# Mixing the last 512 tokens beside the expert turns of the first 512, with the weighted sums as 64x64 corner products

## The chip, the cores and the metric

The kernel runs on one core of one Trainium2 chip. The time is the device time of one launch in microseconds (us), the median of three runs; beside it stands one profiled execution, from which every row below comes.

## The reference

One layer of a hybrid encoder block, batch 1, 1024 tokens, width 1024, float32. It has a token mixer and then a mixture of single-neuron experts (PEER):

```python
h = x @ w_in[l] + b_in[l]                      # conv GLU | q, k, v | two branch gates
y_conv = conformer_conv(h_conv, ...)           # GLU -> causal depthwise conv, 31 taps -> LayerNorm -> silu -> matmul
y_sb = stick_breaking_attention(q, k, v) @ sb_w_o[l]      # 8 heads of 64, strictly causal
mix = (g_conv * y_conv + g_sb * y_sb) @ w_out[l] + b_out[l]
x = layer_norm(DEEPNORM_ALPHA * x + mix, ln1_g[l], ln1_b[l])
# peer, per token and head (8 heads):
s1, s2 = the two halves of (x @ w_q) against 128 keys each; top 16 of each; top 16 of the 256 sums
act = gelu(x . expert_u[idx]);  y += softmax(top)[k] * act[k] * expert_v[idx[k]]      # 16 experts per head
x = layer_norm(DEEPNORM_ALPHA * x + y, ln2_g[l], ln2_b[l])
```

Each of the 1024 tokens picks 8 x 16 = 128 experts, and each expert is a row of 2048 floats (u and v side by side, `uv`), 8 KB.

## The kernel before

Tokens lie in reversed order, in 8 blocks of 128 (one token per partition), so block b attends to the keys of blocks b to 7: block 0 (the last tokens) to eight blocks, block 7 to its own alone. The program is written engine by engine, with semaphores by hand. It has these stages, one after the other:

1. Projections (`split_products`, L171 to L173: each product of two floats as three fp32r products of rounded parts), the depthwise convolution on DVE, and the values.
2. Attention: `UNITS` are the pairs of heads times the blocks, 4 x 8 = 32. For each unit and head, PE makes the scores (L531), ACT two sigmoids (L811, L814), DVE a scan (L1048, `tensor_tensor_scan`, over the unit's width of up to 1024) and a product (L1052), PE turns the result block by block (L546) and multiplies it with the values (L560).
3. Mixing: for each of 8 groups m of 128 output columns and each of two halves h of 512 tokens, PE makes two gates by split products and two branches by plain f32 products (L595); ACT and DVE combine them.
4. `w_out` for block 0 (L607), layer norm 1 (`x1_block`, L1112), queries, scores, top 16.
5. The expert turns: 64 turns (8 blocks x 8 heads) of 8 steps g with two experts each. GpSimd gathers an expert's rows for the 128 tokens of the block with an indirect DMA of 1 MB (L454) into one of 8 slots of `ring`. DVE makes the dot product with x1 (L1173, `dots`) and, in the same turn, the top 16 of the next turn; ACT makes gelu, weight and a diagonal matrix `diag` (L910 to L919, `expert_weights`); PE adds diag x v-row to the block's sum `y` (L649, `experts`), after which the slot is free for the next gather. Turns 0 to 6 also hold `w_out` and layer norm 1 of blocks 1 to 7.

An f32 product of 128x512 shows as two records in the trace (two passes), an fp32r one as one. Names like arena_low and arena_high are the two halves of one big buffer in which nearly all tiles lie; what a row is about is seen from its line. The queue of SP issues the other loads in program order, each behind its semaphore wait.

## Time and profile before

| | |
|---|---|
| median of 3 runs | 3465.28 us (3461.51 to 3466.24) |
| the profiled execution's own time | 3461.93 us |
| its span | 3460.1 us |
| PE, DVE, ACT, POOL busy | 85%, 66%, 36%, 39% of the span |
| moved by DMA | 1134.06 MB, 1073.81 MB of it by the gathers |
| first gather issued, last sum done | 798.1 us, 3449.9 us |

The shares are means over stages with different limits; the table by stage and the rows of single waits say more. A busy PE is not a PE at its peak, since the ends of matmuls are modelled.

### The profile page before, as it was taken

The page shows a single profiled execution, that of the slowest core. Times are in us where ns is not written, and L with a number is a line of the kernel's source. Part 1 is how long each engine was busy: PE and PEld are TensorE (multiplying, and loading weights), DVE is VectorE, ACT ScalarE, POOL GpSimd, SP SyncE. Part 2 cuts the span into 40 slices and gives each one's busy share as a digit, 9 for nine tenths or more (in the row PEclk, how much of TensorE's full clock was granted, in tenths as well). Part 3 has the DMA queues.
Part 4 walks back from the last instruction along what each step waited for, and adds up shares of the span by engine and source line. Part 5 has one row for each costly group of instructions (what it writes and reads, how often), then busy time and mean ns, then how long its engine had stood idle before and what let it go on. Part 6 is the DMA issues. An engine that isn't in the chain of part 4 may idle for free. (4 is left out here: it accounts for less than half of the span.)

```text
span 3460.1 us, 37193 instructions
## 1 busy us (share of the span) xinstructions
PE 2948.2 (85%) x8928; PEld 1540.8 (45%) x8928; DVE 2299.5 (66%) x4699; ACT 1239.6 (36%) x3426; POOL 1356.6 (39%) x1191
## 2 busy tenths in 40 slices
PE   8987799987999788888888888888888888888886
PEld 7754466644444334434333443333434433343432
DVE  6976731115777677676777666777776777777675
ACT  3115621103434343333334333333433333333332
POOL 2400000003434454555554455454445545454553
PEclk9998999998999999999999999999999999999999
DMA  3100011127999999999999999999999999999998
GB/s 147 36 0 19 1 37 44 47 97 319 378 384 382 407 422 422 422 418 412 423 421 419 420 414 422 413 422 421 415 420 421 422 417 421 413 421 419 412 422 339
DMA packets 158049, 1134.06 MB, mean 328 GB/s; under 512 B 17553, under 2 KB 17681, under 8 KB 23442
## 3 DMA queue, kind: packets, MB, share of 16 engines
q0 software_dynamic: 147456, 1073.81, 75.2%
q1 hardware_dynamic: 10514, 59.34, 4.5%
q8 instruction: 32, 0.52, 0.1%
q14 instruction: 47, 0.39, 0.0%
HBM read 1128.88 MB, written 4.19 MB: 327 GB/s over the span
## 5 line engine op out<-in xcount | busy, mean ns | idle before, releaser
L649 PE MATMUL ps<-arena_high 128*128 128x512 f32 x4096 | 1916.7, 614 | 402.9 <-ACT arena_high L919 360.8
L454 POOL DMA_INDIRECT arena_high<-uv_dram,idx_now x1024 | 1225.9, 1197 | 1321.3 <-PE ps L649 1130.0
L1173 DVE SCALAR_TENSOR_TENSOR arena_high<-arena_low,arena_high 128x1024 f32<-128x1024 f32 x1024 | 1239.8, 1225 | 574.4 <-DMA arena_high<-uv_dram,idx_now 561.7
L649 PEld LDWEIGHTS ps<-arena_high 128*128 128x128 f32 x4096 | 766.9, 195 | 1426.5 <-issue 858.0
L910 ACT ACTIVATE gcol<-hcol 128x2 f32<-128x2 f32 x512 | 103.7, 203 | 1200.5 <-DVE arena_high L1173 1200.1
L919 ACT ACTIVATE arena_high<-arena_high,wcol 128x128 f32<-128x128 f32 x1024 | 355.2, 394 | 28.4 <-ACT wcol L912 1.2
L449 POOL CAST idx_now<-arena_high 128x8 uint32<-128x8 f32 x128 | 66.0, 516 | 540.6 <-DVE arena_high L1160 540.1
L912 ACT ACTIVATE wcol<-gcol,arena_low 128x1 f32<-128x1 f32 x1024 | 245.7, 286 | 51.9 <-ACT gcol L910 1.5
L625 PE MATMUL ps<-arena_low 128*128 (+1 forms) x1024 | 236.3, 385 | 5.1 <-DMA arena_low<-w_q_dram 2.9
L625 PEld LDWEIGHTS ps<-arena_low 128*128 128x128 f32 x1024 | 197.5, 193 | 61.0 <-issue 35.0
L173 PE MATMUL ps<-x_hi_bytes,w_bytes 128*128 128x512 f32 x512 | 200.7, 392 | 0.0
L1023 DVE SCALAR_TENSOR_TENSOR arena_low<-arena_low,cols 128x1024 f32 x120 | 177.8, 1481 | 17.5 <-DVE arena_low L1019 0.6
L1072 DVE SCALAR_TENSOR_TENSOR arena_low<-ps,cols,arena_low 128x512 f32<-128x512 f32 x16 | 12.0, 751 | 199.1 <-PE ps L595 199.1
L607 PE MATMUL ps<-arena_low 128*128 128x512 f32 x256 | 116.3, 599 | 7.7 <-DMA arena_low<-w_out_dram 7.7
L1048 DVE TENSOR_TENSOR_SCAN arena_low<-arena_low 128x1023 f32<-128x1023 f32 (+7 forms) x64 | 86.5, 1351 | 42.3 <-ACT arena_low L811 42.3
L595 PE MATMUL ps<-arena_low,arena_high 128*128 128x512 f32 x256 | 112.4, 592 | 0.0
L171 PE MATMUL ps<-x_hi_bytes,w_hi_bytes 128*128 128x512 f32 x256 | 100.9, 394 | 12.2 <-DVE x_lo_bytes L1005 9.0
L171 PE MATMUL ps<-x_hi_bytes,w_bytes 128*128 128x512 f32 x256 | 106.5, 416 | 2.9 <-DVE w_bytes L1064 2.9
L173 PEld LDWEIGHTS ps<-x_hi_bytes,w_bytes 128*128 128x128 f32 x512 | 97.1, 190 | 20.3
L910 ACT ACT_TABLE_LOAD x78 | 100.1, 1283 | 6.4 <-DVE arena_high L1173 5.1
L172 PE MATMUL ps<-x_lo_bytes,w_hi_bytes 128*128 128x512 f32 x256 | 100.6, 393 | 0.0
L172 PE MATMUL ps<-x_lo_bytes,w_bytes 128*128 128x512 f32 x256 | 100.4, 392 | 0.0
(132 smaller groups left out, 2269.3 us busy)
## 6 DMA issues: line engine op xcount, KB each, us to landing
arena_high<-uv_dram,idx_now POOLq DMA_INDIRECT x1024
arena_low<-w_q_dram SPq DMA_DIRECT2D x15, 1024.0 KB, 11.1
arena_high<-w_mix_dram SPq DMA_DIRECT2D x8, 1536.0 KB, 6.3
arena_high<-w_proj_dram SPq DMA_DIRECT2D x16, 512.0 KB, 3.3
arena_high<-xT_dram SPq DMA_DIRECT2D x8, 512.0 KB, 7.6
arena_low<-w_out_dram SPq DMA_DIRECT2D x2, 2048.0 KB, 9.6
arena_low<-x_dram SPq DMA_DIRECT2D x8, 512.0 KB
out_dram<-arena_low SPq DMA_DIRECT2D x8, 512.0 KB
```

Of the source, the lines that this page charges most:

```text
L171: nc.tensor.matmul(out, w_hi, x_hi, start=first, stop=False)
L172: nc.tensor.matmul(out, w_hi, x_lo, start=False, stop=False)
L173: return nc.tensor.matmul(out, w_lo, x_hi, start=False, stop=last)
L454: pool.indirect_dma_start(out=ring[:, s % RING, :], out_offset=None, in_=uv_d, in_offset=bass.IndirectOffsetOnAxis(ap=idx_now[:, s:s + 1], ...
L607: last = nc.tensor.matmul(ps[:, 6 + h, :], mix_blk[:, k, :], w_out[:, k, h * HALF:(h + 1) * HALF], start=(k == 0), stop=(k == KD - 1))
L625: last = nc.tensor.matmul(ps[:, 2, 0:2 * P], x1T[:, k, :], w_q[:, place, k, :], start=(k == 0), stop=(k == KD - 1))
L649: last = nc.tensor.matmul(ps[:, y_bank(b) + h, :], diag[:, s % DIAGS, :], ring[:, s % RING, D + h * HALF:D + (h + 1) * HALF], start=False, ...
L910: steps.link(nc.scalar.activation(gcol[:, s0:s0 + 2], hcol[:, s0:s0 + 2], ACT.Gelu))
L912: last = nc.scalar.activation(wcol[:, s:s + 1], gcol[:, s:s + 1], ACT.Copy, scale=gates_flat[:, bass.ds(t * TOPK + s, 1)])
L919: nc.scalar.activation(diag[:, s % DIAGS, :], ident, ACT.Copy, scale=wcol[:, s:s + 1]).then_inc(diag_ready, 1)
L1023: ins = nc.vector.scalar_tensor_tensor(out=conv[:, c, :], in0=conv_in[:, PAD - k:PAD - k + S], scalar=cols[:, bass.ds(c * TAPS + (C_CW + k ...
L1173: last = nc.vector.scalar_tensor_tensor(out=ring[:, s % RING, 0:D], in0=x1[:, b, :], scalar=1.0, in1=ring[:, s % RING, 0:D], op0=ALU.mult, ...
```

## The change

The first 512 tokens (blocks 4 to 7 of the reversed order) go through attention and mixing alone, and their expert turns start then, as turns 0 to 31. `UNITS` keeps only blocks 4 to 7. Attention for blocks 0 to 3 is done inside turns 11 to 21, five steps to a unit of one pair and one block; their gates and branches in the 52 steps after that (the gates now as plain f32 products instead of three split ones), their `w_out` and layer norm 1 in turns 28 to 30, and their expert turns are 32 to 63. `G` is the number of the step, 8 to a turn. ACT computes the sigmoids of that part as tanh.

The weighted sum changes for all 1024 experts: instead of one 128x128 diagonal times 128x512 per half, an expert takes two 64x64 diagonals on 64 partitions. The even expert of a step uses the corners (lo, lo) and (hi, hi) into PSUM banks 0 and 1, the odd one (lo, hi) and (hi, lo) into banks 2 and 3. At the end of a block the odd sum is copied out by ACT (`odd_out`), swapped and added by PE (`merge`), and read by DVE (`y_out`); the banks are no longer double buffered.

Queries and scores are made for several blocks at a time from `slabs` (2048 query weights and 256 keys per partition, 1.18 MB), which are loaded 21 times in all. The weights `w_mix` and `w_out` are loaded twice, once for each half of the tokens. The first half of the early `w_out` is loaded before mixing ends. The loop over turns is written out.

```diff
-UNITS = [(p, b) for p in range(PAIRS) for b in range(NB)]
+UNITS = [(p, b) for p in range(PAIRS) for b in range(BLK, NB)]
 NU = len(UNITS)
 GROUP = 4
+TURNS = NB * PH
+STEPS = TOPK // 2
+ATT0 = 11 * STEPS
+MIX0 = ATT0 + 84
+OUT0 = MIX0 + 52
+UNIT_STEPS = 5
 
...
+SLABS = [(0, h) for h in range(PH)] + [(0, h) for h in range(5)] + [(1, h) for h in range(PH)]
+
+
...
+def slab_in_turn(t):
+
+    if t < 0:
+        return t + 2
+    if t <= 10:
+        return t + 2
+    return t - 30 + PH + 5 if 30 <= t < 30 + PH else None
+
...
+            def load_w_late(m):
+
+                if m >= 2:
+                    sp_eng.wait_ge(branch_late, m - 1)
+                sp_eng.dma_start(w_mix_late[m % 2], w_mix_d[m, :, :]).then_inc(wmix_late_in[m % 2], 16)
...
+            sp_eng.wait_ge(z_late, 2 * last_unit + 2)
+            sp_eng.dma_start(xT_late, xT_d[:, :, 1, :]).then_inc(xT_late_in, 16)
+            sp_eng.wait_ge(att_late_done, 2 * last_unit + 2)
+            sp_eng.wait_ge(turned_late, 4 * last_unit + 2)
+            load_w_late(0)
+            sp_eng.wait_ge(turned_late, 4 * last_unit + 4)
+            load_w_late(1)
+            load_w_late(2)
+            load_w_late(3)
+            sp_eng.wait_ge(idx_ready, START + 3 * PH)
+            sp_eng.dma_start(x_in[1], x_d[row_of(BLK):row_of(BLK) + P, :]).then_inc(x_loaded, 16)
+            sp_eng.dma_start(b_out_bc[1], b_out_d.partition_broadcast(P)).then_inc(rows_late_in, 16)
+            sp_eng.dma_start(ln1_g_bc[1], ln1_g_d.partition_broadcast(P)).then_inc(rows_late_in, 16)
+            sp_eng.dma_start(ln1_b_bc[1], ln1_b_d.partition_broadcast(P)).then_inc(rows_late_in, 16)
+            load_w_late(4)
+            store_out(2)
+            for m in range(5, KD):
+                load_w_late(m)
+            sp_eng.wait_ge(branch_late, KD - 1)
+            sp_eng.dma_start(w_out_late[1], w_out_d[:, CC:KD, :]).then_inc(wout_late_in[1], 16)
+            sp_eng.wait_ge(gate_late_psum, 2 * KD)
+            sp_eng.dma_start(w_out_late[0], w_out_d[:, 0:CC, :]).then_inc(wout_late_in[0], 16)
+            load_x(BLK + 1)
+            load_x(BLK + 2)
...
-            def experts(b, t, g):
-                for s in range(2 * g, 2 * g + 2):
-                    pe.wait_ge(diag_ready, t * TOPK + s + 1)
-                    for h in range(2):
-                        last = nc.tensor.matmul(ps[:, y_bank(b) + h, :], diag[:, s % DIAGS, :],
-                                                ring[:, s % RING, D + h * HALF:D + (h + 1) * HALF],
-                                                start=False, stop=False, skip_group_check=True)
-                    last.then_inc(expert_used[s % RING], 1)
...
+            def experts(t, g):
+                lo, hi = slice(0, DH), slice(DH, P)
+                e, o = 2 * g, 2 * g + 1
+                pe.wait_ge(diag_ready, t * TOPK + o + 1)
+                for h in range(2):
+                    cs = slice(D + h * HALF, D + (h + 1) * HALF)
+                    for s, rows, out_rows, bank in ((e, lo, lo, h), (e, hi, hi, h), (o, lo, hi, 2 + h), (o, hi, lo, 2 + h)):
+                        last = nc.tensor.matmul(ps[out_rows, bank, :], diag[rows, s % DIAGS, :], ring[rows, s % RING, cs],
+                                                start=False, stop=False, skip_group_check=True)
+                        if h == 1 and rows == hi:
+                            last.then_inc(expert_used[s % RING], 1)
...
+            def merge(pb):
+
+                pe.wait_ge(odd_copied, pb + 1)
+                for h in range(2):
+                    last = nc.tensor.matmul(ps[:, h, :], swap, pre2[:, h * HALF:(h + 1) * HALF],
+                                            start=False, stop=False, skip_group_check=True)
+                last.then_inc(merged, 1)
+
...
+            def stick_scores(u, hd):
+
+                p, b = late_unit(u)
+                w = (NB - b) * P
...
+                r = slice(hd * DH, (hd + 1) * DH)
+                for c0 in range(0, w, HALF):
+                    c1 = min(c0 + HALF, w)
+                    last = nc.tensor.matmul(ps[:, 4 + c0 // HALF, 0:c1 - c0], qT[0][r, p, b * P:(b + 1) * P],
+                                            kT[r, p, b * P + c0:b * P + c1], start=True, stop=True, skip_group_check=True)
+                last.then_inc(z_late, 1)
+
...
+            def late_gates(m, g, k0, k1):
+
+                if g == 0 and k0 == 0:
...
+                for k in range(k0, k1):
+                    o = g * D + k * P
+                    last = nc.tensor.matmul(ps[:, 4 + g, :], w_mix_late[m % 2][:, o:o + P], xT_late[:, k, :],
                                             start=(k == 0), stop=(k == KD - 1))
...
+            def beside(t, g):
+
+                G = t * STEPS + g
+                u, o = divmod(G - ATT0, UNIT_STEPS)
+                if 1 <= u <= PAIRS * BLK and o == 0:
+                    stick_turns(u - 1, 1, 1)
+                if 1 <= u <= PAIRS * BLK and o == 1:
+                    stick_values(u - 1, 1)
+                if 0 <= u < PAIRS * BLK:
+                    if o == 0:
+                        stick_scores(u, 0)
+                    if o == 2:
+                        stick_scores(u, 1)
+                        stick_turns(u, 0, 0)
+                    if o == 3:
+                        stick_turns(u, 0, 1)
+                    if o == 4:
+                        stick_turns(u, 1, 0)
+                        stick_values(u, 0)
+                if MIX0 <= G < OUT0:
+                    m, o = late_mix(G - MIX0)
+                    if o < 4:
+                        late_gates(m, o // 2, CC * (o % 2), CC * (o % 2 + 1))
+                    elif o < 6:
+                        late_branch(m, o - 4)
+                j, o = divmod(G - OUT0, 4)
+                if 0 <= j < BLK:
+                    wout_mm(BLK + j, 2 * o, 2 * o + 2)
+                if 1 <= j <= BLK and o == 2:
+                    transposes(BLK + j - 1)
...
+            def stick_tanh(u, hd):
+
+                _, b = late_unit(u)
+                w = (NB - b) * P
+                i = 2 * u + hd
+                act.wait_ge(z_late, i + 1)
+                if u >= 1:
+                    act.wait_ge(turned_late, 2 * i - 2)
+                else:
+                    act.wait_ge(starts_late_step, 1)
+                nc.scalar.activation(tanh_late[hd][:, 0:w], ps_flat[:, 4 * HALF:4 * HALF + w], ACT.Tanh,
+                                     scale=0.5).then_inc(tanh_done, 1)
+                if u >= 1:
+                    act.wait_ge(stick_late_done, i - 1)
+                act.wait_ge(tanh_done, i + 1)
+                nc.scalar.activation(rest_late[:, hd, 0:w], tanh_late[hd][:, 0:w], ACT.Identity,
+                                     bias=half_col[:, :], scale=-0.5).then_inc(rest_late_done, 1)
+
...
+            def late_stick(u, hd):
+
+                _, b = late_unit(u)
+                w = (NB - b) * P
+                i = 2 * u + hd
+                dve.wait_ge(rest_late_done, i + 1)
+                if i >= 1:
+                    dve.wait_ge(att_late_done, i)
+                nc.vector.tensor_tensor_scan(stick_late[:, 1:w], rest_late[:, hd, 0:w - 1], starts_late[:, 0:w - 1], 0.0,
+                                             ALU.mult, ALU.add).then_inc(stick_late_done, 1)
+                dve.wait_ge(stick_late_done, i + 1)
+                nc.vector.scalar_tensor_tensor(out=tanh_late[hd][:, 0:w], in0=tanh_late[hd][:, 0:w], scalar=1.0,
+                                               in1=stick_late[:, 0:w], op0=ALU.add, op1=ALU.mult).then_inc(att_late_done, 1)
...
+            def beside(t, g):
+
+                G = t * STEPS + g
+                if G == ATT0:
+                    late_starts()
+                u, o = divmod(G - ATT0, UNIT_STEPS)
+                if 0 <= u < PAIRS * BLK and o in (1, 3):
+                    late_stick(u, o // 2)
+                if MIX0 <= G < OUT0:
+                    m, o = late_mix(G - MIX0)
+                    if o == 5:
+                        late_mixed(m)
+                j, o = divmod(G - OUT0, 4)
+                if 1 <= j <= BLK and o == 0:
+                    if j == 1:
+                        dve.wait_ge(rows_late_in, 48)
+                    x1_block(BLK + j - 1)
```

PE in a turn of the last block of before, from the loop body: L633 are the transposes of a query, and the two rows of L649 behind them are one step's sums, two halves of each of two experts.

```order
1297 L633 MATMUL ps<-arena_high,arena_low 128x128 x2
1298 L647 REGISTER_ALU
1299 L649 MATMUL ps<-arena_high 128x512 x2
1300 L647 REGISTER_ALU
1301 L649 MATMUL ps<-arena_high 128x512 x2
```

PE in the changed kernel where the late attention starts: L809 is a step of corner products, L841 the late scores, L853 the turning of the weights, L866 the late values.

```order
977 L809 MATMUL ps<-arena_high 64x512 x8
978 L841 MATMUL ps<-arena_low 128x512 x2
979 L853 MATMUL ps<-arena_high,arena_low 128x128 x4
980 L809 MATMUL ps<-arena_high 64x512 x8
981 L853 MATMUL ps<-arena_high,arena_low 128x128 x4
982 L809 MATMUL ps<-arena_high 64x512 x8
983 L853 MATMUL ps<-arena_high,arena_low 128x128 x4
984 L866 MATMUL ps<-arena_low 64x128 x8
985 L809 MATMUL ps<-arena_high 64x512 x8
```

A step had four products of 128x512 and now has eight of 64x64 corners by 512, with the late work between steps.

DVE in a turn of before, from one pair of dot products (L1173) to the next, with the index part of the top 16 between:

```order
569 L1173 SCALAR_TENSOR_TENSOR arena_high,hcol<-arena_low,arena_high 128x1024 x2
570 L1149 TENSOR_SCALAR top_i<-top_i 128x16
571 L1150 TENSOR_SCALAR pos_ab<-pos 128x16
572 L1151 TENSOR_SCALAR pos_ab<-pos 128x16
573 L1153 TENSOR_TENSOR arena_low<-pos_ab,iota 128x512
574 L1156 TENSOR_TENSOR arena_low<-arena_low,top_i 128x512
575 L1160 TENSOR_REDUCE arena_high<-arena_low 128x16
576 L1173 SCALAR_TENSOR_TENSOR arena_high,hcol<-arena_low,arena_high 128x1024 x2
```

DVE in the changed kernel, the same part inside the late attention: L1486 is the dot product, L1522 the late scan (printed under the name of its instruction class) and L1525 the product behind it.

```order
845 L1522 SCALAR_TENSOR_TENSOR arena_low<-arena_low 128x895
846 L1525 SCALAR_TENSOR_TENSOR arena_low<-arena_low 128x896
847 L1486 SCALAR_TENSOR_TENSOR arena_high,hcol<-arena_low,arena_high 128x1024 x2
848 L1461 TENSOR_SCALAR top_i<-top_i 128x16
849 L1462 TENSOR_SCALAR pos_ab<-pos 128x16
850 L1463 TENSOR_SCALAR pos_ab<-pos 128x16
851 L1465 TENSOR_TENSOR arena_high<-pos_ab,iota 128x512
852 L1468 TENSOR_TENSOR arena_high<-arena_high,top_i 128x512
853 L1472 TENSOR_REDUCE arena_high<-arena_high 128x16
854 L1486 SCALAR_TENSOR_TENSOR arena_high,hcol<-arena_low,arena_high 128x1024 x2
855 L1522 SCALAR_TENSOR_TENSOR arena_low<-arena_low 128x895
856 L1525 SCALAR_TENSOR_TENSOR arena_low<-arena_low 128x896
```

The scans and products that stood ahead of all turns now stand between the dot products of turns 11 to 20, two of each to five steps.

## Rows read from the trace of the kernel before

**Rows 1.** The page: span, busy times, and DMA in 40 slices.

```profile
span 3460.1 us, 37193 instructions
PE 2948.2 (85%) x8928; PEld 1540.8 (45%) x8928; DVE 2299.5 (66%) x4699; ACT 1239.6 (36%) x3426; POOL 1356.6 (39%) x1191
...
DMA  3100011127999999999999999999999999999998
GB/s 147 36 0 19 1 37 44 47 97 319 378 384 382 407 422 422 422 418 412 423 421 419 420 414 422 413 422 421 415 420 421 422 417 421 413 421 419 412 422 339
```

**Rows 2.** By stage: stretch and length, busy of each engine, then granted clock, DMA share, GB/s.

```profile
277.60:456.90 179.30, 134.53 (x1056) 83.53 (x1056) 131.99 (x129) 120.98 (x241) 0.50 (x2) 0.90 0.00 1
456.90:744.30 287.40, 286.07 (x1024) 193.85 (x1024) 49.48 (x61) 35.23 (x47) 0.00 (x0) 0.99 0.10 38
744.30:798.10 53.80, 31.13 (x80) 18.18 (x80) 18.45 (x47) 7.24 (x11) 0.23 (x2) 0.78 0.48 187
798.10:1134.00 335.90, 311.25 (x797) 148.04 (x798) 236.98 (x517) 136.12 (x357) 141.90 (x128) 0.98 0.95 383
1218.00:3431.00 2213.00, 1858.58 (x4766) 869.70 (x4764) 1578.25 (x3654) 842.95 (x2608) 1113.71 (x991) 0.98 1.01 419
```

**Rows 3.** Timeline of the last turn: start, length, engine, line, then idle before.

```profile
3431.27 1.22 DVE L1173 SCALAR_TENSOR_TENSOR arena_high<-arena_low,arena_high 128x1024 f32<-128x1024 f32 x1 [1.25 <-DMA arena_high<-uv_dram,idx_now]
3433.74 1.23 DVE L1173 SCALAR_TENSOR_TENSOR arena_high<-arena_low,arena_high 128x1024 f32<-128x1024 f32 x1 [1.24 <-DMA arena_high<-uv_dram,idx_now]
...
3446.21 3.70 PE L649 MATMUL ps<-arena_high 128*128 128x512 f32 x8 [1.23 <-ACT arena_high L919]
```

**Rows 4.** Who waited for whom, 1218 to 3431 us: total, times, longest.

```profile
POOL arena_high L454 <- PE ps L649: 943.6, 507, 5.3
...
DVE arena_high L1173 <- DMA arena_high<-uv_dram,idx_now: 504.5, 522, 2.2
```

**Rows 5.** Timeline of DVE in the attention stage, second pair of heads and the third's start.

```profile
330.14 2.29 DVE L1048 TENSOR_TENSOR_SCAN arena_low<-arena_low 128x1023 f32<-128x1023 f32 x1 [2.65 <-ACT arena_low L811]
332.46 1.23 DVE L1052 TENSOR_TENSOR arena_low<-arena_low 128x1024 f32<-128x1024 f32 x1
...
351.74 1.49 DVE L1048 TENSOR_TENSOR_SCAN arena_low<-arena_low 128x639 f32<-128x639 f32 x1 [1.38 <-ACT arena_low L811]
353.27 0.83 DVE L1052 TENSOR_TENSOR arena_low<-arena_low 128x640 f32<-128x640 f32 x1
...
357.77 1.22 DVE L1048 TENSOR_TENSOR_SCAN arena_low<-arena_low 128x511 f32<-128x511 f32 x1 [1.42 <-ACT arena_low L811]
...
372.51 2.29 DVE L1048 TENSOR_TENSOR_SCAN arena_low<-arena_low 128x1023 f32<-128x1023 f32 x1 [2.65 <-ACT arena_low L811]
```

**Rows 6.** Timeline of PE in the attention stage, and one stretch of expert sums.

```profile
312.59 1.09 PE L560 MATMUL ps<-arena_low,arena_high 128*64 128x128 f32 x16
313.62 1.13 PE L531 MATMUL ps<-arena_low 64*128 64x512 f32 x4
314.68 1.10 PE L546 MATMUL ps<-arena_low 128*128 128x128 f32 x8
...
1232.05 7.03 PE L649 MATMUL ps<-arena_high 128*128 128x512 f32 x16
```

**Rows 7.** Timeline between mixing and the first gather.

```profile
744.26 0.34 SPq L366 DMA_DIRECT2D arena_low<-w_out_dram  x1
...
751.89 15.61 PE L607 MATMUL ps<-arena_low 128*128 128x512 f32 x32 [7.66 <-DMA arena_low<-w_out_dram]
```

**Rows 8.** Timeline of DVE, the softmax that ends turns 1 and 6.

```profile
894.43 0.16 DVE L1165 RECIPROCAL rden<-den 128x1 f32<-128x1 f32 x1 [0.37 <-ACT arena_high L904]
...
1132.93 0.16 DVE L1165 RECIPROCAL rden<-den 128x1 f32<-128x1 f32 x1 [1.03 <-ACT arena_high L904]
```

**Rows 9.** The page, group of the expert sums: busy, mean ns, idle before.

```profile
L649 PE MATMUL ps<-arena_high 128*128 128x512 f32 x4096 | 1916.7, 614 | 402.9 <-ACT arena_high L919 360.8
```

**Rows 10.** One line's instructions: the read of a finished block's sum.

```profile
L1185 DVE SCALAR_TENSOR_TENSOR arena_low<-arena_low,ps x8: 1215/1217/1222, 1217.6 to 3449.9; 128x1024 f32<-128x1024 f32 x8
```

1246 lines of the change are left out of this document (697 added, 549 removed).

## The prediction

> **What bounds the kernel now.** I read the table by stage first. The reader is to see two programs in it: up to 798 us the DMA moves little (0 to 0.48 of its time) while PE or DVE work, and from 1218 us on the DMA share is 1.01 at 419 GB/s, the same in nearly every slice [rows 1, 2]. A gather moves 128 x 8 KB = 1.049 MB, and at 419 GB/s that is 2.50 us. The timeline of the last turn, where DVE has nothing but dot products, shows it: they start 2.47 us apart, each after a wait for its gather [rows 3]. The waits say the same of the middle: DVE waits 504.5 us in 2213 us for gathers, 9.1 us per turn. GpSimd waits 943.6 us for PE, but that is for a free slot of the ring with gathers still queued, so PE does not bound there [rows 4]. PE is 84% busy all the same (1858.6 of 2213 us): there is no room for mixing beside the old expert sums.
>
> The turns take (3449.9 - 1217.6)/55.4 = 40.3 us each [rows 10]. The first seven take (1132.93 - 894.43)/5 = 47.7 us: there PE is busy 311 of 336 us with `w_out` and queries beside the sums, and DMA falls to 383 GB/s [rows 2, 8].
>
> **The head shrinks.** Attention takes 42.4 us per pair of heads (330.14 to 372.51), and the last four blocks of a pair begin 27.6 us into it (357.77) [rows 5]. Only those four stay ahead of the turns, so 4 x 27.6 = 110, with the wider first unit's lead 112 us go. Mixing is PE-bound (286.1 of 287.4 us) over 16 pieces of 17.9 us, and half stay: -143.5 [rows 2]. Its weights' rounding and splitting now serve one piece instead of two, but DVE and ACT were busy 49 and 35 us of 287, so twice their share stays covered. Between mixing and first gather, 53.8 us, PE waited 7.66 us for `w_out` [rows 7]; its first half is now there, and the transposes of the queries with their copy fall away: -7 (0 if the load of the second half is late instead). The first gather goes from 798.1 to about 536: **-262**, bounds -250 and -268.
>
> **More bytes in the turns.** They are not free when the DMA share is 1.01. Added behind the first gather: 20 slabs of 1.18 MB (23.6), eight `w_mix` (12.6), x for the gates (2.1), both halves of `w_out` (4.2), three rows of norms (1.6), less 14 query weights of 1.05 MB (14.7): +29.4 MB, at 419 GB/s **+70 us**. The lower bound is 40 (some load falls where DVE is the slower), the upper 85.
>
> **The first turns stop being PE-bound.** Their bytes alone, 18.4 MB, take 43.8 us against 47.7, so 7 x 3.9 = **-27**, if PE has the room, which hangs on the corners.
>
> **The corners.** This is the cost that no row shows: four 64x64 products at a time. An f32 product of 512 columns is two records of (7.03 - 0.61)/15 = 0.43 us, so 0.86 us; a step takes four, 3.4 us. The nearest rows are the two halves of what is combined now. L531 makes two such products on different 64 rows of the array into different banks: four records in 1.13 us, where one after the other would take 1.7 and the latency. L560 makes eight products of 128 columns on different 64 output columns, in turn, into one and the same bank: 16 records in 1.09 us against 1.7 and more [rows 6, 9]. So row halves overlap and column halves overlap, nearly whole. I take the four corners as 0.86 us plus little, a step as 1.8 us instead of 3.4. The bounds are 0.86 us for four (a product's own time) and 3.44 us (no overlap), 6.9 us a step.
>
> With that, PE per step, which lasts 5.0 us by DMA: in the late mixing (52 steps) four f32 products (3.4) and the corners, 5.2, but 14.7 MB of weights stretch these steps to 5.6 us by DMA; in chunk queries and `w_out` the same for half of the steps; in late attention some 1.5 + 1.8. DMA stays the bound, narrowly in the mixing. In steps with nothing beside, PE would be busy 1.8 of 5 us. Should the clock granted fall from 0.98 to its lower level (it was 0.78 in the stretch with waits before the first gather [rows 2]), the corners take 3.6 us, as much as the sums take now, and the DMA covers that too.
>
> **Late attention on DVE.** A head's scan and product cost 3.52 us at width 1024 and 2.32 at 640 [rows 5], 2.92 on average, and 32 of them 93 us, in ten turns (80 steps). The idle of DVE there is 10 x 9.1 = 91 us. So DVE and DMA tie. Behind a late scan stand the next dot products, behind those the weights, the sums, and the free slot, and the ring of eight absorbs only part of the lag. I take **+20**, between 0 and 60. ACT gets tanh, scaling and copies, some 5 us to a unit of 25 us, with 62% idle (843 of 2213 us busy): 0, covered by that idle; the order of its instructions has no table load at the tanh.
>
> **Small ones.** Seven block ends now pass ACT copy, merge, read and clearing in series before PE goes on, some 5 us that the ring mostly covers; DVE waits for scores of chunks; layer norms of four late blocks in 16 steps; more instructions to load, since the turns are written out. Together **+15** (0 to 40). The end gets copy and merge before the last read: **+3**.
>
> **Sum.** 3460.1 - 262 + 70 - 27 + 20 + 15 + 3 = 3279 us of span. The profiled execution's own time is 1.8 us above its span, and the median 3.4 above that: **3284 us**, 5.2% less. The likeliest case alone reaches from 3235 to 3335.
>
> **Rivals.**
> Pairs of corners exclude each other. In L531 the two row halves wrote to different banks, in L560 the same bank was shared by products that used the same rows. The corners (lo, lo) and (hi, hi) use different rows and one bank, which neither row covers. If they take turns, four corners cost two products, 1.72 us, and a step 3.4 as now. Then PE bounds the late mixing (6.8 us a step instead of 5.6, some +50 over 52 steps), `w_out` (+20), the first turns (+10), the chunk queries and attention (+10 each): 3284 + 100 = 3385. For it: nothing in the trace; against it: the one bank in L560.
> The Trainium skill, TensorEngine Tiling (Array Packing), "Restrictions and Gotchas", states exactly this rule: different row tiles cannot access the same PSUM bank at once. By it the sum would be 3385, by the rows 3284; this trace has no case of it.
>
> The late attention holds the turns. Each head passes PE, ACT twice, DVE twice, PE, ACT, PE in fixed steps, between dot products that tie with the DMA. If lags don't heal, its turns take 45 to 47 us rather than 42: +40 to +50, 3330. For it: the tie of 93 against 91 us; against it: a chain that is spread over five steps of 5 us.
>
> The corners do not overlap at all. Every step then takes 6.9 us on PE, 512 steps 3530, and the end is at 536 + 3530 + 15, some 4080 us, slower by 18%. It decides from here: outside the sums PE has about 590 us of other work behind the first gather (165 late gates and branches, 118 late attention, 96 `w_out`, 168 chunk queries, the rest transposes, scores and merges), so the old end is reached at (2914 - 590)/512 = 4.5 us a step, 2.27 us for four corners, 1.5 of them at a time. L531 and L560 stand against it with nearly two at a time each.
>
> **Chances.** The likeliest case 0.68, exclusive pairs 0.14, held by late attention 0.12, no overlap or something else as large 0.06. Range: 3225 to 3400 holds the first three but for their tails, some 0.85. Faster by over 0.2%, which is about what three runs can tell from no change: 0.93, within 0.2%: 0.01, slower 0.06.
>
> **What the profile of after would show.** First gather near 536 us. DMA share near 1 from then to the end, and some 1163 MB moved. Eight corner products (16 records) in about 1.8 to 2 us; 3.4 us would be the exclusive pairs, 6.9 no overlap. PE's busy share in the last 26 turns about 40%. Turns of 43 to 44 us at the start, 41 to 42 in late attention, some 45 in late mixing, 40.3 in the last 26. In late attention DVE without long waits for gathers. The prediction is wrong if the DMA share falls well below 1 over many turns, or if the steps beside mixing wait for PE.

## The result

| | before | after |
|---|---|---|
| median | 3465.28 us | 3285.16 us (4 runs, 3283.15 to 3287.93) |
| ratio to before | | 0.9482, 95% interval 0.947 to 0.9494 |
| span of the profiled execution | 3460.1 us | 3281.3 us |
| first gather, last sum | 798.1, 3449.9 us | 523.2, 3271.6 us |
| head; expert phase; rest | 798.1; 2651.8; 10.2 us | 523.2; 2748.4; 9.7 us |

The kernel got 5.2% faster. The head lost 274.9 us and the expert phase gained 96.6.

The page of the changed kernel, to be laid beside [rows 1] and [rows 9]:

```profile
span 3281.3 us, 37294 instructions
PE 2446.8 (75%) x12464; PEld 998.8 (30%) x12464; DVE 2297.7 (70%) x4704; ACT 1159.3 (35%) x3326; POOL 1326.3 (40%) x1197
...
PEclk9998997888888898889999999997777777777777
DMA  3101226999999999999999999999999999999997
GB/s 142 39 0 65 77 104 272 396 413 420 421 420 405 410 409 375 409 420 410 397 397 419 394 409 412 421 419 421 409 421 421 420 398 421 421 421 402 421 421 313
DMA packets 162792, 1163.71 MB, mean 355 GB/s; under 512 B 17857, under 2 KB 17985, under 8 KB 26178
...
L809 PE MATMUL ps<-arena_high 64*64 64x512 f32 x8192 | 1275.3, 749 | 724.2 <-ACT arena_high L1163 721.2
```

The gathers start three slices earlier than in [rows 1]. Behind that the reader sees more slices below 421 GB/s: a stretch from the 13th to the 25th, and then one slice in four. The expert sums were 4096 records and 1916.7 us and are 8192 records and 1275.3 us.

The same by stage (stretch and length, busy of PE, PEld, DVE, ACT, POOL, then granted clock, DMA share, GB/s). The first three rows are attention, mixing and what lies between mixing and first gather, as in [rows 2]. The next eight are the blocks of eight turns, cut where the line that reads a finished sum starts, and the last is all of them:

```profile
279.70:331.30 51.60, 38.02 (x296) 23.48 (x296) 41.48 (x66) 38.29 (x102) 0.00 (x0) 0.88 0.02 7
331.30:475.30 144.00, 143.94 (x512) 97.43 (x512) 31.74 (x36) 23.66 (x30) 0.00 (x0) 0.99 0.18 66
475.30:523.20 47.90, 28.61 (x109) 19.66 (x109) 18.13 (x45) 3.86 (x7) 0.19 (x1) 0.79 0.39 148
...
523.20:890.40 367.20, 285.84 (x1496) 109.78 (x1496) 248.89 (x560) 131.79 (x399) 159.41 (x153) 0.87 1.00 411
890.40:1225.90 335.50, 260.04 (x1529) 106.30 (x1529) 273.86 (x573) 155.83 (x437) 162.36 (x143) 0.89 1.00 411
1225.90:1588.30 362.40, 284.17 (x1563) 111.86 (x1563) 279.07 (x577) 158.10 (x435) 163.92 (x146) 0.91 1.00 405
1588.30:1960.00 371.70, 338.78 (x1528) 121.66 (x1528) 267.50 (x588) 141.18 (x404) 156.29 (x145) 0.96 0.99 401
1960.00:2299.00 339.00, 256.47 (x1320) 85.31 (x1320) 230.10 (x536) 121.18 (x388) 151.59 (x144) 0.88 1.01 418
2299.00:2623.30 324.30, 188.71 (x1033) 43.84 (x1032) 230.42 (x536) 108.05 (x356) 162.01 (x144) 0.74 1.01 418
2623.30:2947.50 324.20, 186.68 (x1032) 43.42 (x1032) 230.69 (x536) 108.05 (x356) 157.69 (x144) 0.75 1.01 415
2947.50:3271.60 324.10, 184.25 (x1032) 42.99 (x1032) 219.28 (x498) 105.30 (x348) 147.28 (x134) 0.77 0.97 400
523.20:3271.60 2748.40, 1984.93 (x10532) 665.15 (x10532) 1979.81 (x4402) 1029.49 (x3120) 1260.54 (x1151) 0.85 1.00 410
```

The kernel before, cut the same way (its read of a sum stands 22 us behind a block's end, so the cuts are moved by that), first block, fourth block, and the whole phase:

```profile
798.10:1195.60 397.50, 359.63 (x926) 172.25 (x927) 273.05 (x593) 157.30 (x416) 166.21 (x151) 0.97 0.96 386
...
1839.20:2161.40 322.20, 269.73 (x699) 126.56 (x698) 230.68 (x536) 123.33 (x380) 160.46 (x144) 0.98 1.01 419
...
798.10:3449.90 2651.80, 2249.13 (x5760) 1054.30 (x5760) 1878.16 (x4309) 1014.80 (x3066) 1291.58 (x1151) 0.98 1.00 413
```

Read together: the first block went from 397.5 to 367.2 us. The second to fifth went from 322 each to 335.5, 362.4, 371.7 and 339.0. These are the blocks beside which the late tokens are mixed, scored and loaded. The last three are about 2 us longer than before.

The last steps of the program on PE (start, length, engine, line, idle before it), which answer to [rows 3] and [rows 6]:

```profile
3255.09 1.95 PE L809 MATMUL ps<-arena_high 64*64 64x512 f32 x16 [1.29 <-ACT arena_high L1163]
3260.05 2.58 PE L809 MATMUL ps<-arena_high 64*64 64x512 f32 x16 [3.01 <-ACT arena_high L1163]
3264.98 3.45 PE L809 MATMUL ps<-arena_high 64*64 64x512 f32 x16 [2.35 <-ACT arena_high L1163]
3269.61 1.98 PE L825 MATMUL ps<-arena_high 128*128 128x512 f32 x4 [1.18 <-ACT arena_high L1172]
```

A step of eight corner products (16 records) takes 1.95 us where the granted clock is 1.00 (the level of 2.4 GHz) and 3.45 us where it is 0.55 (nearly all of it at the level of 1.2 GHz). Steps start 4.9 to 5.0 us apart, so PE is idle for 1.5 to 3 us of each.

### The profile page after: what moved, and what is told of

The parts are those of the page before. It is cut to its first block and busy times, and to the rows that moved or that the text cites. A ratio compares the mean times of both kernels' runs of the same rounds, so it can differ in the third digit from the quotient of the medians.

```text
span 3281.3 us, 37294 instructions
## 1 busy us (share of the span) xinstructions
PE 2446.8 (75%) x12464; PEld 998.8 (30%) x12464; DVE 2297.7 (70%) x4704; ACT 1159.3 (35%) x3326; POOL 1326.3 (40%) x1197
## 2 busy tenths in 40 slices
DMA packets 162792, 1163.71 MB, mean 355 GB/s; under 512 B 17857, under 2 KB 17985, under 8 KB 26178
## 5 line engine op out<-in xcount | busy, mean ns | idle before, releaser
L809 PE MATMUL ps<-arena_high 64*64 64x512 f32 x8192 | 1275.3, 749 | 724.2 <-ACT arena_high L1163 721.2
L1486 DVE SCALAR_TENSOR_TENSOR arena_high<-arena_low,arena_high 128x1024 f32<-128x1024 f32 x1024 | 1237.2, 1224 | 631.4 <-DMA arena_high<-uv_dram,idx_now 620.8
L809 PEld LDWEIGHTS ps<-arena_high 64*64 64x64 f32 x8192 | 308.3, 156 | 1567.7 <-ACT arena_high L1163 1101.6
L1163 ACT ACTIVATE arena_high<-arena_high,wcol 128x64 f32<-128x64 f32 x1024 | 300.4, 340 | 16.7
L1156 ACT ACTIVATE wcol<-gcol,arena_high 128x1 f32<-128x1 f32 x1024 | 245.7, 287 | 16.8
L778 PE MATMUL ps<-arena_low 128*128 128x512 f32 (+1 forms) x512 | 223.5, 580 | 0.0
L1331 DVE SCALAR_TENSOR_TENSOR arena_low<-arena_high,cols,arena_low 128x1024 f32<-128x1024 f32 x120 | 183.9, 1533 | 4.3
L211 PE MATMUL ps<-x_hi_bytes,w_bytes 128*128 128x512 f32 x384 | 151.0, 393 | 0.0
L778 PEld LDWEIGHTS ps<-arena_low 128*128 128x128 f32 x512 | 93.9, 194 | 140.9 <-issue 124.3
L1486 DVE DVE_READ_ACCUMULATOR arena_high<-arena_low,arena_high 128x1 f32 x1024 | 83.8, 82 | 0.0
L881 PEld LDWEIGHTS ps<-arena_low 128*128 128x128 f32 x256 | 47.7, 196 | 76.8 <-issue 76.7
L1522 DVE TENSOR_TENSOR_SCAN arena_low<-arena_low 128x1023 f32<-128x1023 f32 (+3 forms) x32 | 60.4, 1887 | 14.3 <-ACT arena_low L1194 13.9
```

Of the source, the lines that this page charges most:

```text
L211: return nc.tensor.matmul(out, w_lo, x_hi, start=False, stop=last)
L778: last = nc.tensor.matmul(ps[:, 4 + half, j0 * P:j1 * P], w[:, k, half * P:(half + 1) * P], x1T[:, j0:j1, k, :], start=(k == 0), stop=(k = ...
L809: last = nc.tensor.matmul(ps[out_rows, bank, :], diag[rows, s % DIAGS, :], ring[rows, s % RING, cs], start=False, stop=False, skip_group_c ...
L881: last = nc.tensor.matmul(ps[:, 4 + g, :], w_mix_late[m % 2][:, o:o + P], xT_late[:, k, :], start=(k == 0), stop=(k == KD - 1))
L1156: last = nc.scalar.activation(wcol[:, s:s + 1], gcol[:, s:s + 1], ACT.Copy, scale=gates[:, t % (BLK * PH), s:s + 1])
L1163: nc.scalar.activation(diag[:, s % DIAGS, :], ident64, ACT.Copy, scale=wcol[:, s:s + 1]).then_inc(diag_ready, 1)
```

## The experiments

Eleven kernels were made from the changed one, and the changed one was run once more in the last group, beside the three that differ from it by a few us. The two kernels of the next section ran once each, the others four or five times. A gain or loss in us is counted from the changed kernel's first median, 3285.16 us, where nothing else is said.

### Two corners at a time, and one

Both products of the odd expert go where those of the even one go:

```
-  ((e, lo, lo, h), (e, hi, hi, h), (o, lo, hi, 2 + h), (o, hi, lo, 2 + h))
+  ((e, lo, lo, h), (e, hi, hi, h), (o, lo, lo, h), (o, hi, hi, h))
```

> The odd expert of a step goes through the same two corners and into the same banks as the even one, so that two corners are in use and not four; the sum is the same. If all four corners of the changed kernel work at once (16 records of a step in 1.95 us at full clock, in its trace), a step's records should now take about twice that, 3.4 to 3.9 us at full clock. Theory A (the gathers set the time from the first gather to the end): TensorE has room for it while a turn of 8 steps is at 40.5 us, and only beside the late attention and mixing, where it is busy most of the time already, does it cost something: 3285 to 3330 us in all. Rival B (TensorE sets the pace wherever other work stands beside the experts): 512 steps by 1.7 us less what idle time it had, 3385 us or more. Rival C (the two corners that share a bank were not at once before either): 3285 us and 1.95 us a step as before.

And all of them through one corner (the high 64 rows of the sums are left out; both experts' slots are freed behind their last product):

```
-  ((e, lo, lo, h), (e, hi, hi, h), (o, lo, hi, 2 + h), (o, hi, lo, 2 + h))
+  ((e, lo, lo, h), (e, lo, lo, h), (o, lo, lo, h), (o, lo, lo, h))
...
+                for s in (e, o):
+                    done[s].then_inc(expert_used[s % RING], 1)
```

> All products of a step go through the one corner of the low rows and low columns; the high 64 rows of the gathered data and of the sums are left out. It is the ruler for the corners: nothing overlaps, so 16 records of a step should take 16 by 0.43 us = 6.9 us at full clock, against the 1.95 us of the changed kernel with four corners. Then TensorE is the bound through all 512 steps: 523 + 512 x (6.9 to 7.5) + 10 = 4070 to 4370 us. If products of 64 rows in the same corner overlap or take less than 0.43 us each, it is nearer 3300 us.

Measured, in one run each: 3494.95 us with two corners, 4827.45 us with one. A step on PE, with two corners (timeline):

```profile
3101.05 3.65 PE L809 MATMUL ps<-arena_high 64*64 64x512 f32 x16 [1.14 <-ACT arena_high L1163]
```

and with one:

```profile
3103.86 7.08 PE L810 MATMUL ps<-arena_high 64*64 64x512 f32 x16
```

The same 16 records take 7.08, 3.65 and 1.95 us with one, two and four corners: 1.94 times and 3.6 times as fast. In the two-corner kernel (lo, lo) and (hi, hi) use different rows of the array and always the same bank. If these two took turns, that kernel would have shown 7 us. So the corners are free of each other, a shared bank included, and the ruler of the second expectation (6.9 us for one corner) holds.

The two-corner kernel also says what the corners are worth to the whole change. Its step of 3.65 us is as long as the old one, whose 8 records took 3.70 us [rows 3], and with late attention and mixing beside the turns it needs 3494.95 us, more than the 3465.28 us before the change. By this run the move without the shorter sums would have gained nothing.

The times were far above theory A's 3285 to 3330 us, and above the 4070 to 4370 us for one corner. By blocks (starts of the read of a finished sum, differences in us; the first counts from the first gather at 523.2 us of the changed kernel):

| block | 1 | 2 | 3 | 4 | 5 | 6 | 7 | 8 |
|---|---|---|---|---|---|---|---|---|
| changed kernel | 367 | 335.5 | 362.4 | 371.7 | 339.0 | 324.3 | 324.2 | 324.1 |
| two corners | 411 | 351.8 | 402.9 | 449.6 | 369.2 | 326.5 | 324.8 | 324.8 |
| one corner | 607 | 555.8 | 586.7 | 656.5 | 548.4 | 445.1 | 446.7 | 446.5 |

With two corners the last three blocks cost nothing, as theory A has it: 3.65 us still fits in a step. The first five cost 44, 16, 41, 78 and 30. Beside the late attention PE is then the bound (stretch, then busy of PE first):

```profile
1015.00:1430.00 415.00, 396.20 (x1865) 157.82 (x1864) 338.44 (x682) 198.71 (x527) 200.42 (x170) 0.99 0.97 382
```

It is busy 396 of 415 us and the gathers fall to 382 GB/s. The changed kernel is busy 285.84 of 367.2 us in its first block and 338.78 of 371.7 in its fourth; 64 steps by 1.7 us more, 109 us, fit in neither, nor in the 75 to 83 us that it idles in the second, third and fifth. In each of the last three it idles 136 us or more. So rival B of this expectation (TensorE sets the pace wherever other work stands beside the experts) is right for five blocks and theory A for three.

### More bytes

Twelve loads of the size of a late slab, which nobody reads, in turns 41 to 52:

```
+            for n in range(12):
+                sp_eng.wait_ge(idx_ready, START + 41 + n)
+                sp_eng.wait_ge(slab_in, 16 * (len(SLABS) + n))
+                sp_eng.dma_start(slab[1], slabs_d[n % PH, :, :]).then_inc(slab_in, 16)
...
```

> Twelve loads of the size of a late feature slab (14.2 MB in all), whose data nobody reads, are added in the turns 41 to 52, after the late mixing is done. Theory A (bytes set the time there): 14.2 MB by 1/419 GB/s, about +34 us, 3319 us. Rival B (the pace of a turn is set by an engine or a gather's own latency, and the DMA engines have slack): under +10 us. Rival D (the loads disturb the gathers by more than their bytes): +45 us or more.

Measured: 3319.20 us (3315.62 to 3321.34), ratio 0.9585 (0.9569 to 0.9601), +34.0 us. The sixth and seventh blocks grew from 324.3 and 324.2 to 345.4 and 338.3 us, the eighth did not (322.9). Bytes cost there what 419 GB/s make of them.

### Fewer weights in the late mixing

```
+                n = 3 * D if m < 2 else P
-                sp_eng.dma_start(w_mix_late[m % 2], w_mix_d[m, :, :])
+                sp_eng.dma_start(w_mix_late[m % 2][:, 0:n], w_mix_d[m, :, 0:n])
```

> Of the late copy of the mixing weights only 128 of 3072 columns are loaded from the third group on (6 loads of about 1.5 MB less; the products read what the buffer held before, so the mixed values of the last 512 tokens are not the reference's). Theory A (bytes set the time of the late mixing, 306 us for 52 steps): 9.1 MB by 1/419 GB/s, about -21 us, 3264 us. Rival B (TensorE or ScalarE set it there): within 5 us of the changed kernel.

Measured: 3284.26 us (3282.54 to 3289.43), ratio 0.9492 (0.9477 to 0.9508): no change. First the stretch of the late mixing in the changed kernel, then in this one:

```profile
1465.00:1780.00 315.00, 289.91 (x1244) 100.57 (x1245) 202.08 (x451) 111.47 (x325) 125.83 (x118) 0.96 1.00 405
```

```profile
1465.00:1780.00 315.00, 291.19 (x1252) 100.86 (x1248) 202.88 (x459) 110.19 (x326) 129.01 (x120) 0.96 0.97 379
```

The rate falls from 405 to 379 GB/s, 8.2 MB in 315 us, and the time stays. The late mixing is not bound by bytes, and theory A fell. (Six loads are cut to 128 of 3072 columns each.)

### Half of the late gates

```
-                for k in range(k0, k1):
+                for k in range(k0, k1, 2):
```

> The late gates are made with half of their products (every second block of 128 features is left out, so the mixed values of the last 512 tokens are not the reference's). Theory A (the late mixing, 306 us for 52 steps, goes at the pace of the bytes): within 5 us of 3285 us. Rival B (TensorE sets the pace there, since it has gates and experts in the same steps): about -30 to -45 us, 3240 to 3255 us.

Measured: 3277.35 us (3271.03 to 3278.65), ratio 0.9455 (0.9441 to 0.947), -8 us. The stretch:

```profile
1465.00:1780.00 315.00, 254.36 (x1167) 82.09 (x1168) 214.06 (x486) 115.43 (x341) 138.87 (x126) 0.93 1.01 421
```

Two groups of instructions say how long the mixing itself took, the late gates and the branches: first and last start in the changed kernel, with durations,

```profile
L881 PE MATMUL ps<-arena_low x256: 592/592/1220, 1468.9 to 1764.7; 128*128 128x512 f32 x128
L895 PE MATMUL ps<-arena_low x128: 592/592/697, 1491.1 to 1775.7; 128*128 128x512 f32 x128
```

and with half of the gates:

```profile
L881 PE MATMUL ps<-arena_low x128: 592/592/1220, 1468.9 to 1748.2; 128*128 128x512 f32 x128
L895 PE MATMUL ps<-arena_low x128: 592/592/697, 1487.7 to 1759.7; 128*128 128x512 f32 x128
```

The mixing took 290.8 us in place of 306.8, and now it goes at 421 GB/s. So neither expectation was met: PE bounds it in the changed kernel, with the DMA 16 us behind, and half of the gates is more than it takes to change the bound.

Only 8.4 of these 16 us are left at the end of the fourth block. Most of the others are lost again in the late `w_out` products that stand right behind the mixing, first in the changed kernel, then in this one:

```profile
L739 PE MATMUL ps<-arena_low x128: 592/592/697, 1778.6 to 1870.3; 128*128 128x512 f32 x128
L739 PE MATMUL ps<-arena_low x128: 592/592/697, 1765.9 to 1861.0; 128*128 128x512 f32 x128
```

From the last branch to the last of these it is 94.6 us in the changed kernel and 101.3 with half of the gates. One reason can be read from the bytes. During its mixing the changed kernel moved 124.17 MB, this one 122.35; the 1.8 MB, 4.3 us at 421 GB/s, are gathers that ran ahead into the ring while PE was the bound, and that this kernel has still to make. The blocks behind the fourth are together 5 us longer in this trace, the slowest of the four executions; why, it doesn't show.

### A short scan in the late attention

```
-  tensor_tensor_scan(stick_late[:, 1:w], rest_late[:, hd, 0:w - 1], starts_late[:, 0:w - 1], ...)
+  tensor_tensor_scan(stick_late[:, 1:64], rest_late[:, hd, 0:63], starts_late[:, 0:63], ...)
```

and the product behind it in the same way.

> The scan and the product behind it of the late attention cover 64 columns in place of up to 511 (the rest of the weights is left out, so the late half is not the reference's). Theory A' (VectorE sets the pace beside the late attention, 5.31 us a step against 5.06 us a step in the undisturbed turns; about 77 steps): -15 to -20 us, 3265 to 3270 us. Rival B' (the gathers and the late scores' own loads set it there): within 4 us of the changed kernel. Rival C' (TensorE, which also makes the late scores, sets it): within 4 us too, and the idle time of VectorE in 1015 to 1430 us is then put down to TensorE.

Measured: 3274.13 us (3266.64 to 3276.28), ratio 0.9454 (0.944 to 0.9469), -11 us. The stretch in the changed kernel and in this one:

```profile
1015.00:1430.00 415.00, 320.55 (x2004) 136.93 (x2000) 370.39 (x731) 215.62 (x568) 211.90 (x178) 0.90 0.99 402
```

```profile
1015.00:1430.00 415.00, 322.27 (x2072) 138.39 (x2070) 306.64 (x751) 219.85 (x582) 204.15 (x185) 0.92 1.01 416
```

Who waited for whom there (total, times, longest), two lines of the changed kernel and the same two of this one:

```profile
ACT gcol L1154 <- DVE arena_high L1486: 168.5, 56, 7.2
DVE arena_high L1486 <- DMA arena_high<-uv_dram,idx_now: 18.2, 18, 2.6
...
ACT gcol L1154 <- DVE arena_high L1486: 162.5, 68, 4.9
DVE arena_high L1486 <- DMA arena_high<-uv_dram,idx_now: 93.1, 93, 2.2
```

DVE was busy 370.4 of 415 us in the changed kernel, and the gathers went at 402 GB/s. With 64 us of scan taken away they go at 416. ACT's wait for the dot products is about the same in both and tells nothing; DVE's own wait for gathers does: 18 us with the full scan, when the data were nearly always there first, and 93 us without it. PE has the same work in both (320.6 and 322.3 us), so rival C' is out. Theory A' holds in kind: what the late attention costs the turns is DVE's time. Its size, 15 to 20 us, is less sure. The late mixing starts at 1449.9 us in place of 1468.9, and the execution in the trace ended 16.5 us before that of the changed kernel; but it is the fastest of the four, and by the medians the gain is 11.

### The clock

```
+                    if t >= 38:
+                        for _ in range(7):
+                            nc.tensor.matmul(ps[:, 7, :], zeros[:, 0:P], zeros[:, :], start=True, stop=True, ...)
```

> From turn 38 on TensorE makes seven products of zeros more in each step (128 x 512, bf16, into a bank that nothing uses then), so that it is not idle long enough for its granted clock to fall to 0.7 to 0.8. Theory A (the fallen clock costs nothing, since the gathers set the pace): the same time within 3 us, with a granted clock near 1.0 in the last third. Rival B (the low clock lengthens the part of a step that is on the path): -5 to -15 us. Rival C (the added products delay the expert products behind them): +5 us or more.

Measured: 3286.58 us (3280.81 to 3288.35), ratio 0.9483 (0.9469 to 0.9498). The last third in the changed kernel and in this one:

```profile
2260.00:3250.00 990.00, 568.14 (x3152) 132.07 (x3144) 698.36 (x1615) 329.18 (x1088) 484.93 (x439) 0.76 1.01 417
```

```profile
2260.00:3250.00 990.00, 718.85 (x4520) 224.00 (x4516) 700.03 (x1622) 328.73 (x1086) 504.64 (x440) 0.98 1.01 417
```

The granted clock goes from 0.76 to 0.98 and neither rate nor time moves. A step's sums at the lower clock are hidden too, and the fallen clock is free.

### What a block's end costs

The last three blocks take 324.2 us, and the sixth and seventh go at 418 and 415 GB/s where single slices reach 421: 2.3 and 4.6 us of each are below full rate. Four kernels looked for them. The first, in its core, has banks of its own for every second block from the sixth on, and the last sum of a block stands behind the first step of the next:

```
+def y_bank(pb):
+    return 4 if pb in (5, 7) else 0
...
+                    if own and t % PH == 0 and g == 1:
+                        merge(t // PH - 1)
```

> From the sixth block of expert turns on, every second block sums into the banks 4 to 7, which the late mixing has left free by then, and the closing of a block (merge, the copy of the odd half, the last sum) stands behind the first step of the next block and not ahead of it. Theory A (a turn is 39.8 us by its bytes, and the closing of a block makes some 4.5 us of every 324 us in which the gathers wait for buffers): -9 to -13 us for the three block ends, 3272 to 3276 us. Rival B (the buffers of the gathers cover the closing, and 40.5 us a turn is the pace of the DMA engines): within 3 us of 3285 us.

Measured: 3288.33 us (3283.31 to 3295.42), ratio 0.9495 (0.9482 to 0.9508). No gain where theory A had 9 to 13 us: what PE's wait for the last sum costs is too little to measure, as rival B had it. The trace of the changed kernel then showed another thing. Here is DVE (third of the busy times) and the rate (last column) 27 us before a block's end at 2947.5 us, and in the 40 us behind it:

```profile
2920.00:2930.00 10.00, 7.38 (x32) 1.60 (x32) 7.08 (x13) 5.47 (x15) 2.66 (x4) 0.50 1.02 423
...
2950.00:2960.00 10.00, 6.78 (x48) 1.61 (x40) 9.55 (x29) 2.54 (x10) 3.26 (x4) 0.83 0.99 388
2960.00:2970.00 10.00, 5.12 (x36) 1.26 (x32) 8.42 (x18) 6.90 (x16) 4.43 (x5) 0.83 0.97 367
2970.00:2980.00 10.00, 3.12 (x24) 0.81 (x18) 9.45 (x16) 3.91 (x12) 3.15 (x4) 0.73 1.01 416
2980.00:2990.00 10.00, 6.49 (x48) 1.82 (x44) 5.30 (x14) 2.54 (x10) 5.82 (x7) 0.84 0.93 354
```

DVE is busy 84 to 96% for 30 us behind the block's end, with the read of the sum, the choice of the next experts and the closing norm, and in three of four slices the gathers fall to 354 to 388 GB/s. The next kernels act on the norm. One leaves most of it out at three block ends:

```
+                w = 16 if 4 <= pb < NB - 1 else D
```

> The norm that closes a block covers 16 of 1024 columns for the fifth to the seventh block (the other columns are stored without it), which takes some 4 us of VectorE out of the fifth step after each of these three block ends. Theory N (a block takes 324.2 us and not 320 because VectorE is 93 to 96% busy in the 40 us behind its end, where the norm stands beside the choice of the next experts, and dots come late, so that the gathers fall from 421 to 350 to 400 GB/s): -6 to -12 us for the three, 3273 to 3279 us. Rival S (the store of the block and its writes cost the DMA engines that time): within 2 us of the unchanged kernel. Rival B (the wait of TensorE for the last sum costs it): within 2 us too.

The other cuts it in four, a piece to each of the steps 4 to 7:

```
-                    if t % PH == 0 and t >= 1 and g == 4:
-                        finish(t // PH - 1)
+                    if t % PH == 0 and t >= 1 and g >= 4:
+                        finish_part(t // PH - 1, g - 4)
```

> The norm that closes a block is cut into four pieces, one in each of the steps 4 to 7 of the turn behind the block's end, where VectorE has only the two dots (about 2.6 of 5.06 us). Theory N: -1 to -2.5 us for each of seven block ends, -5 to -15 us, 3270 to 3280 us. Rival S or B: within 2 us of the unchanged kernel.

The last has both, the cut norm and the own banks, with the sum's read moved to step 4:

```
+                    if t % PH == 0 and t >= 1 and g == (4 if own else 0):
                         y_out(t // PH - 1)
```

> As the kernel with the cut norm, and from the sixth block on each second block has banks of its own, so that the last sum of a block waits until step 4 of the next turn and the norm follows in the steps 5 to 7; nothing of a block's end then stands beside the choice of the next experts. Theory N: 3 to 6 us less than the kernel with the cut norm alone (two to three block ends by 1 to 2 us each), 3265 to 3277 us. Rival B (only TensorE's wait counts): the cut norm alone gives nothing and this one gives 3 us, as own banks alone did in their last block.

And the changed kernel beside them:

> The changed kernel itself once more, as the ruler for the three kernels beside it, which differ from it by a few us only: 3285 us within 3 us.

| | median | runs | ratio to before |
|---|---|---|---|
| changed kernel again | 3288.02 | 3280.61 to 3293.95 | 0.9492 (0.9476 to 0.9509) |
| norm left out at three ends | 3285.26 | 3282.34 to 3288.60 | 0.9486 (0.9473 to 0.9499) |
| norm cut in four | 3277.12 | 3274.88 to 3281.89 | 0.9466 (0.9453 to 0.9479) |
| cut, own banks, later read | 3275.79 | 3272.45 to 3280.19 | 0.9459 (0.9446 to 0.9472) |

Cutting the norm gives 11 us, 0.33%, as expected, against the repeated kernel (8 against the first four runs; its slowest run, 3281.89 us, overlaps the fastest of the repeated kernel). But the kernel without the norm at three ends gives 3, not 6 to 12, which is less than its spread. The stretch behind the fifth block's end has the dip in the repeated kernel,

```profile
2299.00:2349.00 50.00, 26.17 (x159) 6.76 (x161) 39.79 (x95) 17.17 (x52) 20.54 (x20) 0.77 0.96 383
```

and without the norm it has none:

```profile
2299.00:2349.00 50.00, 29.14 (x160) 7.36 (x164) 37.22 (x97) 18.44 (x58) 21.68 (x23) 0.79 1.01 422
```

The block is stored inside this stretch in both (the store is issued at 2326.9 and 2324.7 us), so at this end the store is not the cause (rival S). In the 50 us behind the two other ends the rate is 391 and 412 GB/s without the norm and 375 and 378 with it. Measured against 421 GB/s, the three stretches together lose 15 us with the norm and 5 without. Yet the sixth, seventh and eighth blocks take 326.5, 321.4 and 324.7 us, against 326.8, 325.3 and 323.7 in the repeated one: one end gives 3.9 back and the two others nothing. So a dip of the rate is not yet time of the kernel, and most of the 10 us that the dips lost less are lost elsewhere. Nor do single blocks tell much here: the sixth took 324.3 us in one execution of the changed kernel and 326.8 in the other. The blocks of the kernel with the cut norm say where its gain is. The third takes 359.5 us against 362.8 and the fourth 367.9 against 372.8, where PE or DVE bound anyway; from the fifth on it is 1.7, 2.7, 1.3 and -1.2. So the norm's place costs something, and by this one pair of traces most of it in the loaded blocks. What the ends of the last three cost is not settled. The own banks add 1 us to the cut norm, not the 3 to 6 expected, and that is nothing measurable.

## Why the prediction was right

**The time** came out 1.2 us from the forecast, which is partly luck: the head gave 13 us more than I summed and the expert phase took 16 more.

**The head: -262 forecast, -274.9 measured.** Mixing gave 287.4 - 144.0 = 143.4 us against 143.5, and what lies behind it 53.8 - 47.9 = 5.9 against 7. The wait of 7.66 us for `w_out` [rows 7] is gone:

```profile
477.52 14.00 PE L739 MATMUL ps<-arena_high,arena_low 128*128 128x512 f32 x32 [2.24 <-DVE arena_low L1388]
```

The mis-sized term is the attention, "112 us go". Mixing starts at 331.3 us in place of 456.9, so 125.6 went. A pair of heads takes 11.9 us, from the first scan to the next pair's:

```profile
292.35 1.22 DVE L1356 TENSOR_TENSOR_SCAN arena_high<-arena_high,arena_low 128x511 f32<-128x511 f32 x1 [1.37 <-ACT arena_high L1051]
...
304.24 1.22 DVE L1356 TENSOR_TENSOR_SCAN arena_high<-arena_high,arena_low 128x511 f32<-128x511 f32 x1 [1.37 <-ACT arena_high L1051]
```

I had left it the 14.8 us that the last four blocks took before [rows 5]. In them were waits of DVE for ACT of 1.48, 0.27 and 2.65 us, the last before the next pair's wide start; now they are 0.27 and 1.37. I had carried an interval over with its waits in it.

**Bytes: +70 forecast.** The page has 1163.71 MB, as forecast (1163). In the turns it is 410 x 2748.4 against 413 x 2651.8 us, 31.7 MB more, which at 421 GB/s is +75. The extra loads confirm the price, +34.0 us for 14.2 MB.

**The rest of the expert phase** is time in which the DMA engines ran below full rate. Worked out as length by (1 - rate/421): before 33 us in the first block, 8 in the next six and 10 in the last; after 8.7, 8.0, 13.8, 17.7, 2.4, 2.3, 4.6 and 16.2, together 74 against 51, so +23. With the bytes that is +98, against 96.6 measured. My terms for it were -27, +20, +15 and +3, together +11; the bytes gave 5 more than their +70.

- *The first turns, -27*: 33 - 8.7 = 24 us went. The step holds, and it does hang on the corners: with two of them the block takes 44 us more.
- *Late attention on DVE, +20*: DVE and DMA tie, as I wrote, and the short scan shows it from DVE's side with 11 us. The size holds too: 402 in place of 421 GB/s over the 415 us is 19 us. From the first late score (1015.2 us) to the first late gate (1468.9) it is 84 steps at 43.2 us a turn. That lies between my 41 to 42 and the 45 to 47 us of the rival "the late attention holds the turns", which did not come.
- *The step that failed* is "DMA stays the bound, narrowly in the mixing", with 5.6 us a step. PE was the bound at 5.9 us: six smaller loads changed nothing, fewer products did, and with half of the gates the steps took the 5.6 us (290.8/52) that I had for the bytes. The error is small in time, 0.3 us in 52 steps, 16 us, and large as a reading, since all my trust in hidden PE time rested on it. My 5.2 us for PE counted gates, branches and corners; the stretch has PE busy 289.91 of 315 us, 92%, which leaves no cover for a lag of the others.
- *Small ones, +15*: I named block ends, "some 5 us that the ring mostly covers". The merge's wait is covered, as the own banks show. What costs something is the norm's place on DVE behind them, 11 us by the cut norm over all seven ends, which I had not seen. The last block loses 16.2 us against 10 before, and the late `w_out` and norms go at 381 GB/s (1850 to 1900 us); no run took these apart.

**The corners**, 1.8 us a step: 1.95. Row halves and column halves overlap at once, as the two nearest rows had it one by one [rows 6].

**The rival "pairs of corners exclude each other"** is out, by 1.95 us and by the two-corner kernel. By this trace the rule of the Trainium skill (TensorEngine Tiling (Array Packing), "Restrictions and Gotchas") that different row tiles can't use one PSUM bank at once does not show up as time here: (lo, lo) and (hi, hi) share a bank and 16 records take half of what one corner takes.

**The prices of the two corner rivals were too low.** I gave +100 and 4080 us; two corners cost +210, one corner 4827. In the second I forgot my own number: outside the sums PE has about 590 us of other work. 523 + 512 x 7.08 + 590 + 10 = 4748 is near the measured time, and the sum without the 590 is not; where the last 79 us come from I can't say. In the first I gave 10 us each to the first turns, the chunk queries and the late attention; the first three blocks, where most of these stand, cost 44, 16 and 41. PE had less room there than I thought: what 109 us more are above its idle time in the changed kernel, block by block, is 28 + 34 + 31 + 76 + 26 = 195 us, near the measured 210.

**The clock** fell to 0.74 to 0.77 in the last three blocks. I had written that DMA covers that, and the kernel that keeps it up confirms it. My 40% for PE's busy share in the last 26 turns left it out: it was 57%.

**The signs of being wrong.** One of the two came: the steps beside the mixing waited for PE. The other, a DMA share well below 1, did not, but with 0.99 to 1.01 in stages with three different bounds that share can't tell.

## What to carry to other kernels

When a change makes one engine's part shorter in a stage that the DMA bounds, its value lies in the cover that it gives to other work moved there: four corners in place of two gained next to nothing in the last three blocks and 210 us in the first five, and with two the move would have made the kernel slower. Price what is moved beside a bound with the sum of busy times of each engine per step, and take a share near 90% for a bound (DVE at 89% and PE at 92% were), whatever the DMA's share says: 0.99 to 1.01 stood in the stages that PE, DVE or the gathers bounded alike. An engine with room on average can be full for 30 us; look at the rate in short windows behind regular events, and spread what stands there over the light steps (11 us here). But test it, since a dip that is gone need not be time won.

## What the runs showed of the hardware

- Sixteen records of 64 x 512 f32 take 7.08, 3.65 and 1.95 us with one, two and four corners of the array, although in the two-corner kernel both write one PSUM bank, and with four each pair does.
- The DMA share in the stage table doesn't tell bound from unbound: in the late mixing it read 1.00 at 405 GB/s and, with fewer weights and the stage no slower, 0.97 at 379. In the last blocks 1.01 went with 415 to 418. The rate beside the 421 of full slices tells more.
- The granted clock was 0.76 in 990 us in which PE was busy 57%, and 0.98 when it was busy 73% with products of zeros added, and the kernel took the same time.
